# Two transformer blocks on one core: the second block's q and k rows turned by DMA instead of by TensorE

## The reference

```python
h = rmsnorm(x, norm_mix_g)
proj = h @ w_in                       # 2048 x 8704
qa, ka, va, qb, kb, vb, ga, gb = jnp.split(proj, IN_OFFSETS, axis=-1)
# widths: 1024, 256, 256, 1024, 1024, 1024, 2048, 2048
ya = sliding_window_attention(qa, ka, va, sinks) @ w_branch_a   # 16 q heads, 4 k/v heads of 64
yb = stick_breaking_attention(qb, kb, vb) @ w_branch_b          # 16 heads of 64
merged = sigmoid(ga) * ya + sigmoid(gb) * yb
x = x + merged @ w_out
```

## Time and profile before

| | us |
|---|---|
| median of 3 runs | 2591.73 (2590.72 to 2591.82) |
| the profiled execution's own time | 2592.41 |
| its span in the profile | 2590.66 |
| TensorE busy | 2545.8 (98% of the span) |
| VectorE busy | 1675.1 (65%) |
| ScalarE busy | 1293.9 (50%) |
| GpSimd busy | 220.4 (9%) |

### The profile page before, as it was taken

One profiled execution on the slowest core, in us unless ns is written; L12 is line 12 of the kernel. 1 busy time (PEld: TensorE's weight loads), 2 busy tenths in 40 slices (PEclk: granted clock), 3 DMA queues, 4 the chain that ended last, 5 costly groups with the idle time before them and its releaser, 6 DMA issues.

```text
span 2590.7 us, 31484 instructions
## 1 busy us (share of the span) xinstructions
PE 2545.8 (98%) x11482; PEld 2068.3 (80%) x11482; DVE 1675.1 (65%) x1867; ACT 1293.9 (50%) x1620; POOL 220.4 (9%) x269
## 2 busy tenths in 40 slices
PE   6999999999999999999999999999999999999998
PEld 2788888878888888888888877788888888888887
DVE  4987878968777766555544485756655555555454
ACT  3444456445555554444544465654555555554443
POOL 0030132300000000000100042301000000000000
PEclk7999999999999999999999999999999999999999
DMA  9997987968988777676666545456676767676654
GB/s 395 386 335 260 330 260 250 344 210 270 273 262 269 217 219 211 187 210 203 189 209 192 174 140 152 147 194 202 197 216 201 208 198 213 194 216 201 193 194 156
DMA packets 355536, 587.87 MB, mean 227 GB/s; under 512 B 106196, under 2 KB 106572, under 8 KB 354924
## 3 DMA queue, kind: packets, MB, share of 16 engines
q1 hardware_dynamic: 329488, 514.92, 63.6%
q0 software_dynamic: 18928, 69.39, 7.7%
q10 hardware_dynamic: 7020, 2.26, 0.6%
HBM read 563.94 MB, written 2.10 MB: 218 GB/s over the span
## 4 chain that ended last, share of the span: by engine, by line
PE 88%; DMA 5%; DVE 4%; issue 1%; ACT 1%; SPq 0%; POOL 0%; DVEq 0%; ACTq 0%
PE gp L1527 28%; PE gp L1529 28%; PE gp L1528 28%; DMA raw<-in_w_in_dram 2%; DMA proj<-in_w_ada_dram 2%; DVE w_lo L2008 2%; DMA raw<-in_w_up_dram 1%; DMA ada_ring<-in_w_ada_dram 1%; DVE ada_sum L2135 1%; ACT w_hi L891 0%; PE tp L1768 0%; PE tp L1882 0%; PE tp L1758 0%; PE tp L1967 0%; PE tp L1822 0%
## 5 line engine op out<-in xcount | busy, mean ns | idle before, releaser
L2008 DVE TENSOR_TENSOR w_lo<-raw,w_hi 128x1024 fp32r<-128x1024 f32 x872 | 1076.0, 1238 | 779.5 <-ACT w_hi L891 775.9
L891 ACT CAST w_hi<-raw 128x1024 fp32r<-128x1024 f32 x872 | 912.2, 1051 | 976.2 <-PE gp L1529 776.8
L1527 PE MATMUL gp<-w_hi,h_hi 128*128 128x512 f32 x2656 | 1047.6, 394 | 7.8 <-DVE w_lo L2008 5.5
L1529 PE MATMUL gp<-w_hi,h_lo 128*128 128x512 f32 x2656 | 1035.4, 390 | 0.0
L1528 PE MATMUL gp<-w_lo,h_hi 128*128 128x512 f32 x2656 | 1035.0, 390 | 0.0
L1527 PEld LDWEIGHTS gp<-w_hi,h_hi 128*128 128x128 f32 x2656 | 499.3, 188 | 119.9 <-DVE w_lo L2008 12.1
L1529 PEld LDWEIGHTS gp<-w_hi,h_lo 128*128 128x128 f32 x2656 | 499.1, 188 | 105.6
L1528 PEld LDWEIGHTS gp<-w_lo,h_hi 128*128 128x128 f32 x2656 | 499.5, 188 | 101.2 <-issue 0.2
L1527 PE MATMUL gp<-w_hi,a_hi 128*128 128x512 f32 x704 | 274.3, 390 | 0.0
L1528 PE MATMUL gp<-w_lo,a_hi 128*128 128x512 f32 x704 | 273.9, 389 | 0.0
L1529 PE MATMUL gp<-w_hi,a_lo 128*128 128x512 f32 x704 | 273.9, 389 | 0.0
(11 more groups left out here) (320 smaller groups left out, 1396.0 us busy)
## 6 DMA issues: line engine op xcount, KB each, us to landing
raw<-in_w_in_dram SPq DMA_DIRECT2D x248, 512.0 KB, 4.5
raw<-in_w_up_dram SPq DMA_DIRECT2D x176, 512.0 KB, 4.6
raw<-in_w_ffn_in_dram SPq DMA_DIRECT2D x176, 512.0 KB, 4.3
ada_ring<-in_w_ada_dram POOLq DMA_DIRECT2D x128, 512.0 KB, 5.9
raw<-in_w_down_dram SPq DMA_DIRECT2D x88, 512.0 KB, 4.8
raw<-in_w_ffn_down_dram SPq DMA_DIRECT2D x88, 512.0 KB, 4.6
proj<-in_w_ada_dram SPq DMA_DIRECT2D x64, 512.0 KB, 10.4
raw<-in_w_out_dram SPq DMA_DIRECT2D x64, 512.0 KB, 5.4
```

The source lines that it names most:

```text
L891: nc.scalar.copy(w_hi[:, s], raw[:, s]).then_inc(hi_ready, 1)
L1527: mm(o, hi[:, kt0 + kt, ps], w_hi[:, s, k, :], start=n == 0, stop=False)
L1529: return mm(o, lo[:, kt0 + kt, ps], w_hi[:, s, k, :], start=False, stop=n == g.kts - 1)
L2008: V.tensor_tensor(w_lo[:, s], raw[:, s], w_hi[:, s].bitcast(F32), ALU.subtract).then_inc(lo_ready, 1)
```

## The change

TensorE's 56 transposes, ScalarE's 14 copies from PSUM and VectorE's doubling copies of k are removed. In their place, for chunks 0 to 6 of `g_in2a` (1024 columns qa, 256 ka with 256 va, 1024 qb, 1024 kb), while the following chunks are multiplied:

- VectorE copies the drained chunk into two 16-bit planes in `gates2` (block 4 of the next chunk). For chunk 2 it takes ka only and doubles it in this copy (four smaller copies);
- SyncE waits for the planes and issues two transposing DMAs (block 7 of the next chunk) into a buffer in `gates2`;
- ScalarE and VectorE each join one half (block 1 of the chunk after that) back into the chunk's own columns of `proj2`, or into `K2` for chunk 2.

The scores read `proj2` directly (`pair_tile`), and the outputs overwrite the q tile of their head pair. The factor 1/8 of kb moves from ScalarE's copies to the drains of chunks 5 and 6 (`rows2k`, one more small VectorE instruction). In the diff, the first `between` is ScalarE's, `mixers` TensorE's, the second `between` VectorE's. `g_in2a` is unrolled on ScalarE, VectorE and SyncE (before: a hardware loop). The mixers start at k = 1 and k = 22 instead of 7 and 37, and end after k = 43.

```diff
-        SW0 = 7
+        SW0 = 1
         SK0 = SW0 + HS + 5
-        SK1 = SK0 + 9
+        SK1 = SK0
...
+        qk_turn = gates2[:, 1, 0:2 * CW].bitcast(U16).rearrange("p (q s) -> p q s", s=S)
+        K_CHUNK = KA2 // CW
+        QK_TURNS = VS2 // CW
+
+        def qk_planes(t):
+            return gates2[:, 0, t * CW:(t + 1) * CW].bitcast(U16).rearrange("p (w n) -> p w n", w=2)
+
+        def qk_rows(c_, t):
+            return proj2[:, t, c_ * CW:(c_ + 1) * CW].bitcast(U16).rearrange("p (n w) -> p w n", w=2)
+
+        def qk_half(c_, w):
+
+            if c_ == K_CHUNK:
+                return K2.bitcast(U16).rearrange("p f (s w) -> p f s w", w=2)[:, :, :, w]
+            return proj2[:, :, c_ * CW:(c_ + 1) * CW].bitcast(U16).rearrange(
+                "p a (b s w) -> p a b s w", b=2, w=2)[:, :, :, :, w]
+
+        def qk_turn_half(c_, w):
+            a = qk_turn[:, 4 * w:4 * w + 4, :]
+            return a if c_ == K_CHUNK else a.rearrange("p (a b) s -> p a b s", a=2)
...
+        def pair_tile(a, p):
+
+            return a[:, (p % 4) // 2, (p // 4) * 2 + p % 2]
...
+            def turn_qk(i, e, j, first):
+                c_ = 2 * i + e - 1
+                if 0 <= c_ < QK_TURNS and j == 7:
+                    sp.wait_ge(qk_ready, ST * (c_ + 1))
+                    if c_:
+                        sp.wait_ge(qk_joined, 2 * c_)
+                    for t in range(ST):
+                        sp.dma_start_transpose(qk_turn[:, :, t * P:(t + 1) * P],
+                                               qk_planes(t).rearrange("p w n -> p (w n)")).then_inc(qk_turned, 16)
...
             def between(i, e, j, first):
+                m = 2 * i + e - 2
+                if 0 <= m < QK_TURNS and j == 1:
+                    act.wait_ge(qk_turned, 16 * ST * (m + 1))
+                    nc.scalar.copy(qk_half(m, 1), qk_turn_half(m, 1)).then_inc(qk_joined, 1)
...
             def mixers(k):
-                if k < 6:
-                    n = k
...
-                    for a in range(2):
-                        for t in range(ST):
...
-                            last = nc.tensor.transpose(tp[:, n % 4, a * S + t * P:a * S + (t + 1) * P], src,
-                                                       ident[:, :])
-                if SK0 <= k < SK0 + 8:
...
-                            last = nc.tensor.transpose(tp[:, n % 4, a * S + t * P:a * S + (t + 1) * P],
-                                                       proj2[:, t, col + a * P:col + (a + 1) * P], ident[:, :])
...
             def between(i, e, j, first):
+                c_ = 2 * i + e - 1
+                if 0 <= c_ < QK_TURNS and j == 4:
+                    for t in range(ST):
+                        dve.wait_ge(drained[t], g_in2a.chunk0 + c_ + 1)
+                        if c_ == K_CHUNK:
+                            for u in range(2):
+                                o = qk_planes(t).rearrange("p w (g u d) -> p w g u d", g=HK, u=2)[:, :, :, u]
+                                last = V.tensor_copy(o, ka[:, t].bitcast(U16).rearrange(
+                                    "p g (d w) -> p w g d", w=2))
+                        else:
+                            last = V.tensor_copy(qk_planes(t), qk_rows(c_, t))
+                        last.then_inc(qk_ready, 1)
+                m = c_ - 1
+                if 0 <= m < QK_TURNS and j == 1:
+                    dve.wait_ge(qk_turned, 16 * ST * (m + 1))
+                    V.tensor_copy(qk_half(m, 0), qk_turn_half(m, 0)).then_inc(qk_joined, 1)
...
+                    link(V.tensor_tensor(rows2[:, :], rstd[:, 2, :], rstd[:, 3, :], ALU.mult))
+                    V.tensor_scalar(rows2k[:, :], rows2[:, :], DH ** -0.5, None, ALU.mult
                                     ).then_inc(rows_ready, 1)
...
+                    r = rows2k if g is g_in2a and KS2 <= (2 * i + e) * CW < VS2 else rows
```

More of the change, by code:

```diff
@@ L199, in two_blocks @@
         rrow = junk[:, 0:S]
-        sb("to_line", [P, 8])
+        rows2k = sb("rows2k", [P, ST])
+        sb("to_line", [P, 6])
         VC = {"c": 0, "g1": 16, "g2": 32, "mixg": 48, "ffng": 64, "ghead": 80, "gfin": 88}
@@ L446, in two_blocks @@
         sink_landed = sem("sink_landed")
-        q2_t = sem("q2_t")
-        q2_c = sem("q2_c")
-        kdup_ready = sem("kdup_ready")
+        qk_ready = sem("qk_ready")
+        qk_turned = sem("qk_turned")
+        qk_joined = sem("qk_joined")
         sw_s = sem("sw_s")
@@ L717, in _ @@
                 stream(g, nxt, turn_up if g is g_up else turn_down if g is g_down
-                       else turn_out2 if g is g_out2
+                       else turn_out2 if g is g_out2 else turn_qk if g is g_in2a
                        else turn_pair if g is g_up2 else None)
@@ L1318, in drain @@
                         act.wait_ge(rows_ready, 1)
+                    r = rows2k if g is g_in2a and KS2 <= (2 * i + e) * CW < VS2 else rows
                     nc.scalar.activation(dst[:, 0, bass.ds(i * 2 * CW + e * CW, CW)], gp[g.bank(e)][:, 0, :],
-                                         ACT.Identity, scale=rows[:, 0:1]).then_inc(drained[0], 1)
+                                         ACT.Identity, scale=r[:, 0:1]).then_inc(drained[0], 1)
                 return drain
@@ L1331, in between @@
                     root(3)
-            stream(g_in2a, scaled_drain(g_in2a, proj2, rows2), each=between, nxt=g_in2b, peel=True)
+                m = 2 * i + e - 2
+                if 0 <= m < QK_TURNS and j == 1:
+                    act.wait_ge(qk_turned, 16 * ST * (m + 1))
+                    nc.scalar.copy(qk_half(m, 1), qk_turn_half(m, 1)).then_inc(qk_joined, 1)
+            stream(g_in2a, scaled_drain(g_in2a, proj2, rows2), each=between, nxt=g_in2b, unrolled=True)
             act.preload_act_table_set("natural_log_exp_and_others")
             def mixers(k):
-                if k < 6:
-                    n = k
-                    act.wait_ge(q2_t, n + 1)
-                    dst = Q2[:, 2 * n:2 * n + 2] if n < 4 else K2[:, 2 * (n - 4):2 * (n - 4) + 2]
-                    nc.scalar.copy(dst, tp[:, n % 4, :].rearrange("p (a s) -> p a s", a=2)).then_inc(q2_c, 1)
                 if SW0 <= k < SK0:
@@ L1399, in mixers @@
                         act.wait_ge(o2_mm, HS + h + 1)
-                        nc.scalar.copy(OS[:, h // 8, (h // 2) % 4], tp[:, 3, 0:S]).then_inc(o2_out, 1)
+                        nc.scalar.copy(pair_tile(OS, h // 2), tp[:, 3, 0:S]).then_inc(o2_out, 1)
             def mixed_high(kps=range(4, NP8)):
@@ L1888, in mixers @@
             def mixers(k):
-                if k < 6:
-                    n = k
-                    if n == 0:
-                        for t in range(ST):
[L1895 to L1899, removed]
-                    for a in range(2):
-                        for t in range(ST):
-                            src = (proj2[:, t, QA2 + (2 * n + a) * P:QA2 + (2 * n + a + 1) * P] if n < 4 else
-                                   kdup[:, t, 2 * (n - 4) + a].rearrange("p u d -> p (u d)"))
-                            last = nc.tensor.transpose(tp[:, n % 4, a * S + t * P:a * S + (t + 1) * P], src,
-                                                       ident[:, :])
-                    last.then_inc(q2_t, 1)
                 if SW0 <= k < SK0:
@@ L1910, in mixers @@
                         if h == 0:
-                            pe.wait_ge(q2_c, 6)
+                            pe.wait_ge(qk_joined, 2 * (K_CHUNK + 1))
                         else:
@@ L1915, in mixers @@
                         for u in range(2):
-                            mm(tp[:, u, 0:P], Q2[half(u), h // 2, 0:P], K2[half(u), g, 0:P], start=True, stop=True)
+                            mm(tp[:, u, 0:P], pair_tile(OA, h // 2)[half(u), 0:P], K2[half(u), g, 0:P],
+                               start=True, stop=True)
                         for u in range(2):
-                            last = mm(tp[:, u, P:SW_N], Q2[half(u), h // 2, P:S], K2[half(u), g, :],
+                            last = mm(tp[:, u, P:SW_N], pair_tile(OA, h // 2)[half(u), P:S], K2[half(u), g, :],
                                       start=True, stop=True)
@@ L1950, in mixers @@
                         if h == 0:
-                            pe.wait_ge(q2_c, 14)
+                            pe.wait_ge(qk_joined, 2 * QK_TURNS)
                         else:
@@ L1954, in mixers @@
                         for u in range(2):
-                            mm(tp[:, u, 0:P], Q2[half(u), h // 2, 0:P], K2[half(u), h // 2, 0:P],
-                               start=True, stop=True)
+                            mm(tp[:, u, 0:P], pair_tile(OS, h // 2)[half(u), 0:P],
+                               pair_tile(KS, h // 2)[half(u), 0:P], start=True, stop=True)
                         for u in range(2):
-                            last = mm(tp[:, u, P:SW_N], Q2[half(u), h // 2, P:S], K2[half(u), h // 2, :],
-                                      start=True, stop=True)
```

(8 more changed lines are left out.)

17 lines of the change are left out of this document (4 added, 13 removed).

## The result

The changed kernel took 2603.69 us (median of 13 runs, 2602.09 to 2607.68) against 2593.11 us (13 runs, 2590.25 to 2605.06) for the kernel before: a ratio of 1.0042, 95% interval 1.0034 to 1.0051. The forecast was 2584.8, faster by 0.27%; it is slower by 0.42%. The profiled execution took 2603.32 us, its span is 2601.6 us against 2590.7, so 10.9 us have to be found, or rather 17.9, if the forecast's 7 us (6.96) were gained as well.

What follows compares the result with a forecast made beforehand. TensorE, busy 2545.8 of 2590.7 us, was taken as the bound. Removed 6.76, gained 0.2 and added 0 gave 2591.73 - 6.96 = 2584.8 us, 0.27% less, with a range of 2582.6 to 2588.2.

Steps and rivals of the forecast that it cites:

- added 0: In the sum: the new copies, joins, DMA turns and unrolled code cost TensorE nothing, 0 us.
- The groups of transposes: On TensorE: removing 14 groups of four saves 0.486 us each for six and 0.481 for eight, 6.76 us.
- the lost wait: Sliding-window stage: a 0.3 us TensorE wait perhaps goes with the drain on its second head; 0.2 us gain taken.
- The copies on the other engines: VectorE and ScalarE: new copies and joins, 2.13 and 1.354 us a chunk, fit in idle time and stay hidden.
- The unknown copies of chunk 2: VectorE: four half-size copies, a pattern not in the trace, take between 1.4 and 2.7 us; 2.7 taken, hidden.
- A (drains on heavy steps): Mixers: drains on ScalarE's heavy steps or VectorE's delay TensorE, up to 2.0 us, 2586.8 us; 13%.
- B (the turns starve the weights): SyncE's queue: transposing DMAs make weight loads late, TensorE waits about 2 us a turn, 2599 us; 6%.
- ScalarE's waits for loads: Sign of being wrong: waits of `w_hi` for a DMA in `g_in2a` in the new profile.
- The prediction's 10 us: SyncE's queue in `g_in2a`: a weight load may be about 10 us late before TensorE waits.
- the Trainium skill's rule: Turn 128x128 tiles on TensorE where PSUM allows; by its figures, 21.8 us of TensorE swapped for 147 of DMA.
- C (full duration): On TensorE: the transposes cost their full 272 ns each, so 15.2 us go, 2576.5 us; 2%.
- D (the startup waits vanish): Stick-breaking stage: its 1.4 us of TensorE waits at the start go too, 2583.4 us; 7%.

Runs made afterwards that it cites:

- b_shift32: The kernel before with only the filler `to_line` made 32 bytes larger, moving every tensor behind it; 2610.05 us against 2593.33, ratio 1.0065.
- a_line: The changed kernel without the 24-byte filler `to_line`, so tensors behind it return to their old addresses; 2584.88 us, ratio 0.9974 to the kernel before.
- a_plus56: The changed kernel without the filler, plus 14 groups of four 128x128 transposes whose results nobody reads; 2593.07 us, ratio 0.9994 to the kernel before.
- a_late: The changed kernel without the filler, with mixers at their old places, k = 7 and 37; 2585.74 us, ratio 0.9973 to the kernel before.
- a_turn2: The changed kernel without the filler, each transposing DMA issued twice, the second into an unused buffer; 2587.83 us, ratio 0.9967 to the kernel before.
- a_turn4: The changed kernel without the filler, each transposing DMA issued four times, extra copies into unused buffers; 2611.93 us, ratio 1.0067 to the kernel before.

## Why the prediction was wrong

**The step that failed** is "added 0" in the sum, and the sentence that it rests on: "work taken from TensorE comes off the end one for one, as long as nothing it waits for gets later". Nothing that TensorE waits for got later, and still its own matmuls in `g_down`, `g_out2` and `g_down2` took 0.2333 us instead of 0.2267. The tacit assumption was that products outside the changed stage keep their rate; the prediction gave no reason for it and looked for slower matmuls in `g_in2a` alone. The sum had no entry for where tensors lie. The diff showed the cause openly, a new tensor and a filler cut by the same number of bytes, and the filler's name says what it is for; I read it as a balance and didn't ask for the granularity of the allocation. No rival covered it either. The missing term is 2496 matmuls by 0.00667 us, 16.6 us; `b_shift32` measures it as 16.7, and the changed kernel stands 2603.69 - 2584.88 = 18.8 us above `a_line`, by medians. The 2 us more lie ahead of `g_down` in the two traces, whose first matmul starts at 1018.4 and 1016.4 us.

**What held.** The groups of transposes: 6.76 us forecast, the stage 7.0 us shorter where the sum with the 0.2 us of the lost wait was 6.96, and `a_plus56` gives it all back. The copies on the other engines cost TensorE nothing; here they are after, with the turn (durations as in the earlier trace rows; the third and fourth rows are groups, busy us and mean ns; the DMAs landed in 3.2 to 4.5 us):

```profile
L2608 DVE COPY gates<-proj x12: 682/689/690, 1301.5 to 1428.7; 128x1024 uint16<-128x1024 uint16 x12
L1371 ACT COPY proj<-gates x6: 1352/1363/1364, 1311.8 to 1440.4; 128x1024 uint16<-128x1024 uint16 x6
L2613 DVE COPY proj<-gates 128x1024 uint16<-128x1024 uint16 x6 | 4.5, 753 | 0.0
L2605 DVE COPY gates<-proj 128x512 uint16<-128x512 uint16 x4 | 1.4, 421 | 0.0
L737 SPq DMA_TRANSPOSE gates<-gates x14: 1243/1290/2061, 1302.8 to 1430.7; - x14
```

The unknown copies of chunk 2 last 4 x 0.421 = 1.7 us and, since they overlap, hold VectorE for 1.4 us. That is the lower of the prediction's bounds, 1.4 and 2.7, and not the upper one that it took.

**The rivals.** A (drains on heavy steps): not seen, `a_late` is the same within the interval. B (the turns starve the weights): not at this size. ScalarE's waits for loads, one of the prediction's signs of being wrong, did grow, from 3.2 us over two blocks before to 8.3 over four after, but TensorE doesn't notice. `a_turn2` and `a_turn4` put the point where it turns between 5.3 and 10.7 us of queue time a turn. The prediction's 10 us less 1.4 of waiting, 8.6, lies between them; the tests don't fix it more closely. By the Trainium skill's rule ("VectorE: DVE Perf Modes", "Rules for kernel authors") the transposes would have stayed on TensorE; `a_line` at 0.9974 goes against it here, where TensorE is the bound and the DMAs have room. C (full duration) is out. D (the startup waits vanish) is out: 0.9 and 0.4 us are still there.

**Left open.** Why a start off a multiple of 256 bytes costs a matmul 16 clock periods (at 32 or 64 bytes; none between 128 and 256 and no shift below 32 was tried), why 128 bytes cost a little less, and whether two operands off their places cost twice; no run moved both.

## What to carry to other kernels

When a kernel that TensorE bounds gets a new tensor, work out the start address of every matmul operand behind it, with the allocator's own rounding, before anything else: here 32 bytes cost more than twice what the change gained. A slower product of this kind showed neither in busy shares nor in waits nor in the granted clock. Count the matmuls of a stretch, compare the mean duration of each group of matmuls, or take the distance between starts, also in stages that the change doesn't touch. And a step that moves work from the bounding engine to a queue can be trusted once its reserve is worked out in us and tested by doubling the load; here that reserve held, and the price beyond it was underestimated by half.

## What the hardware did that I had not expected

- A 128x128 by 128x512 float32r matmul took 0.2267 us from start to start with both operands' tensors starting at multiples of 256 bytes in the partition, 0.2333 us with the stationary or the streamed one 32 bytes off (the stationary one: 64 off the same), and 0.2324 with the stationary one 128 off.
- The profile's busy share and granted clock are the same in both cases (180.00 of 180 us, 1.00); the count of matmuls differs (796 and 773), and so does a matmul's mean duration (390 and 396 ns).
